# Gated linear attention inside a three-block kernel: the seven score levels of a 128-token tile become three levels of four blocks and one halving

## What is computed

```python
proj = h @ w_in                                    # q, k, v, r, gk_low; 4 heads, keys 128 wide, values 256 wide
log_a = log_sigmoid(gk_low @ w_gk_up + b_gk) / 16.0
b = cumsum(log_a) within a chunk
o_inter = einsum(q * exp(b), state)
attn[i, j] = sum_k q[i, k] * k[j, k] * exp(b[i, k] - b[j, k])   for j <= i
o_intra = attn @ v
state = state * exp(b_last) + (k * exp(b_last - b)).T @ v
y = (rms_norm(o_inter + o_intra) * silu(r)) @ w_out
```

## Time and profile before

| | us |
|---|---|
| median of three runs | 2564.52 |
| profiled execution, device time | 2564.55 |
| its span, first to last instruction | 2562.7 |
| GLA from t = 4 of head 1 to its last attend, 1532.58 to 1770.23 | 237.65 |
| of it TensorE busy | 237.65 |

### The profile page before, as it was taken

One profiled execution on the slowest core, in us unless ns is written; L12 is line 12 of the kernel. 1 busy time (PEld: TensorE's weight loads), 2 busy tenths in 40 slices (PEclk: granted clock), 3 DMA queues, 4 the chain that ended last, 5 costly groups with the idle time before them and its releaser, 6 DMA issues.

```text
span 2562.7 us, 34944 instructions
## 1 busy us (share of the span) xinstructions
PE 2527.1 (99%) x12568; PEld 2131.8 (83%) x12568; DVE 1220.7 (48%) x2483; ACT 922.5 (36%) x1840; POOL 467.0 (18%) x934
## 2 busy tenths in 40 slices
PE   8999999999999999999899999999999999999999
PEld 7888888888888987788788888888888888888887
DVE  4553634536423410577755767765443333333334
ACT  5443433324313422555544545443331122112212
POOL 3453534434000304322010001101000000000001
PEclk9999999999999999999999999999999999999999
DMA  6220212202533121222343111123331111111111
GB/s 211 78 76 22 93 36 64 67 27 85 192 115 111 63 95 48 60 60 60 98 146 113 40 61 34 41 74 114 109 140 41 50 57 41 47 44 64 33 49 74
DMA packets 76232, 194.48 MB, mean 76 GB/s; under 512 B 8528, under 2 KB 29392, under 8 KB 75344
## 3 DMA queue, kind: packets, MB, share of 16 engines
q1 hardware_dynamic: 76112, 192.85, 22.8%
HBM read 152.45 MB, written 36.18 MB: 74 GB/s over the span
## 4 chain that ended last, share of the span: by engine, by line
PE 58%; DVE 2%; issue 1%; ACT 1%; DMA 0%; POOL 0%; DVEq 0%; ACTq 0%; POOLq 0%
PE wc_g_ps L3431 14%; PE wc_y_ps L3447 14%; PE gl_vr_ps L2568 7%; PE gl_j_ps L2527 3%; PE wb_y_ps L2898 3%; PE wc_y_ps L3180 3%; PE gl_l_ps L2594 2%; PE at_T_ps L1931 1%; PE at_j_ps L1886 1%; PE at_v_ps L1886 1%; PE at_j_ps L1887 1%; PE at_j_ps L1888 1%; PE at_v_ps L1887 1%; PE at_v_ps L1888 1%; PE at_s_ps L1888 1%
## 5 line engine op out<-in xcount | busy, mean ns | idle before, releaser
L3431 PE MATMUL wc_g_ps<-x_upper,ff_w1l 128*128 128x512 f32 x512 | 199.3, 389 | 0.0
L3431 PE MATMUL wc_g_ps<-x_upper,ff_w1h 128*128 128x512 f32 x512 | 199.2, 389 | 0.0
L3447 PE MATMUL wc_y_ps<-ff_w2h,ff_hl 128*128 128x512 f32 x512 | 199.2, 389 | 0.0
L3447 PE MATMUL wc_y_ps<-ff_w2l,ff_hh 128*128 128x512 f32 x512 | 199.2, 389 | 0.0
L3431 PE MATMUL wc_g_ps<-x_lower,ff_w1h 128*128 128x512 f32 x512 | 199.2, 389 | 0.0
L3447 PE MATMUL wc_y_ps<-ff_w2h,ff_hh 128*128 128x512 f32 x512 | 199.2, 389 | 0.0
L3385 DVE TENSOR_TENSOR ff_acc<-wc_y_ps,ff_acc 128x1024 f32<-128x1024 f32 x63 | 77.2, 1225 | 210.9 <-PE wc_y_ps L3447 210.9
L3310 ACT ACTIVATE ff_relu<-wc_g_ps 128x512 f32<-128x512 f32 x64 | 38.3, 598 | 379.4 <-PE wc_g_ps L3431 379.4
L3371 DVE SCALAR_TENSOR_TENSOR wc_g_ps<-wc_g_ps,ff_relu 128x512 f32<-128x512 f32 x64 | 44.8, 700 | 178.7 <-ACT ff_relu L3310 178.7
L3339 POOL TENSOR_SCALAR ff_ms<-ff_ss 128x1 f32<-128x1 f32 x8 | 1.8, 223 | 686.9 <-ACT x_lower L3327 686.0
L3447 PEld LDWEIGHTS wc_y_ps<-ff_w2h,ff_hl 128*128 128x128 f32 x512 | 96.1, 188 | 20.0
(11 more groups left out here) (442 smaller groups left out, 6998.2 us busy)
## 6 DMA issues: line engine op xcount, KB each, us to landing
staging<-in_w_ff SPq DMA_DIRECT2D x64, 512.0 KB, 3.7
ra_raw<-in_w_wide_a SPq DMA_DIRECT2D x24, 512.0 KB, 3.7
ra_raw<-in_w_narrow_a SPq DMA_DIRECT2D x16, 512.0 KB, 3.7
staging<-in_w_vr_c SPq DMA_DIRECT2D x16, 512.0 KB, 3.9
wa_gin<-gated_a SPq DMA_DIRECT2D x6, 1024.0 KB, 4.9
ra_first_raw<-in_w_wide_a SPq DMA_DIRECT2D x8, 512.0 KB, 8.0
ra_x_rows<-in_x SPq DMA_DIRECT2D x8, 512.0 KB, 5.3
gated_a<-ra_sg SPq DMA_DIRECT2D x32, 128.0 KB, 2.0
```

Of the source, the lines that this page charges most:

```text
L3431: last = pe.matmul(f_ps[j % 2][:, :], a[kt // 2][:, kt % 2, f * P:(f + 1) * P], b[:, kt, half * HALF:(half + 1) * HALF], start=(kt == 0 an ...
L3447: last = pe.matmul(y_ps[t % 2][:, n, :], a[:, f, t * P:(t + 1) * P], b[f][:, n * HALF:(n + 1) * HALF], start=(f == 0 and i == 0), stop=(f ...
```

## The change

Six of the seven levels are joined by two: blocks of 1, 4 and 16 tokens, in groups of four blocks. Within a group every later block is scored against each earlier one, with reference r = 0, 1, 2 the last token of block r. The queries behind reference r are 96, 64 and 32 columns for a tile, 192 for each level; the keys of a level need one row of 128. For blocks of one token the keys are k itself. One halving (64 against 64) is left. The diagonal is taken from a product of k and q as they are, 128 columns. The exponents of a half are now 3·4·192 + 2·512 + 512 = 3840 instead of 4096, and `KD` moves to `lv_rest`, in place of q·k. Since k and q are now read directly and are overwritten for the next head before the last tiles are scored, tiles 4 to 7 get copies, `own_qk`. Four instructions of 256 elements make them in `products(h, 1)`. The scores lie in `l_ps` (128 + 192 + 192) and in `T_ps` (192 + 64 + 128 for the transpose). `gather_weights` has eleven parts in place of eight. The square in `output` now writes to `o_ps` instead of `osq`, whose place the copies take, and `attend` waits for `sq_done` instead of `o_copied`. In the closing product row 3 waits also for the scores of the last head's tile 3, and some tiles of the closing product and the feed-forward network change places.

```diff
-GLA_LEVELS = 7
+GLA_BLOCKS = (1, 4, 16)
+GLA_HALF = 64
...
+    BY_REF = (0, 96, 160)
+    QUERIES = 192
+    PARTS = 3 * NL + 2
+    LEVEL_AT = (P, P + QUERIES, 0)
+    HALVES_AT, KEYS_AT = QUERIES, QUERIES + GLA_HALF
...
+    def by_reference(c, level, r):
+
+        n = GLA_BLOCKS[level]
+        return queries(c, level)[:, :, BY_REF[r]:BY_REF[r] + 32 * (3 - r)].rearrange("p t (g x) -> p t g x", x=(3 - r) * n)
...
-            act.activation(lv_main[c][:, :, :], lv_main[c][:, :, :], ACT.Exp, scale=INV_NORM)
+            act.activation(lv_main[c][:, :], lv_main[c][:, :], ACT.Exp, scale=INV_NORM)
+            act.activation(lv_rest[c][:, 1, :], lv_rest[c][:, 1, :], ACT.Exp, scale=INV_NORM)
...
-            act.activation(osq[:, :], oS[:, t % 2, :], ACT.Square, accum_out=so[:, t % 2:t % 2 + 1]).then_inc(sq_done, 1)
+            act.activation(o_ps[:, 0:GV], oS[:, t % 2, :], ACT.Square, accum_out=so[:, t % 2:t % 2 + 1]).then_inc(sq_done, 1)
...
-            for level in range(NL):
-                n = 1 << level
-                src = b[:, at].rearrange("p (g u n) -> p g u n", u=2, n=n)
-                dst = lv_main[c][:, level, :].rearrange("p (g u n) -> p g u n", u=2, n=n)
-                mid = src[:, :, 0, n - 1:n].broadcast_to([P, HALF // (2 * n), n])
-                dve.tensor_tensor(dst[:, :, 0, :], mid, src[:, :, 0, :], ALU.subtract)
-                dve.tensor_tensor(dst[:, :, 1, :], src[:, :, 1, :], mid, ALU.subtract)
+            for level, n in enumerate(GLA_BLOCKS):
+                if level:
+                    src = b[:, at].rearrange("p (g n) -> p g n", n=n)
+                    dve.tensor_tensor(keys(c, level).rearrange("p (g n) -> p g n", n=n),
+                                      src[:, :, n - 1:n].broadcast_to([P, HALF // n, n]), src, ALU.subtract)
+                for r in range(3):
+                    src = b[:, at].rearrange("p (t g x) -> p t g x", t=BT, x=4 * n)
+                    dve.tensor_tensor(by_reference(c, level, r), behind_reference(b[:, at], level, r),
+                                      src[:, :, :, (r + 1) * n - 1:(r + 1) * n].broadcast_to([P, BT, 32 // n, (3 - r) * n]),
+                                      ALU.subtract)
...
+            if c:
+                for src in (q, k):
+                    for i in range(2):
+                        dve.tensor_copy(own_qk[src is k][i][:, :, :],
+                                        src[:, HALF + 2 * i * P:HALF + 2 * (i + 1) * P].rearrange("p (t n) -> p t n", n=P))
+            dve.tensor_tensor(lv_rest[c][:, 1, :], lv_rest[c][:, 1, :], k[:, at], ALU.mult)
+            dve.tensor_tensor(lv_rest[c][:, 0, :], lv_rest[c][:, 0, :], q[:, at], ALU.mult).then_inc(mul_done, 1)
...
+            dve.copy_predicated(aT_parts[0][:, :], ident[:].bitcast(U32), l_ps[:, 0:P]).then_inc(part_done, 1)
+            dve.copy_predicated(aT_parts[1][:, GLA_HALF:], mask[:, MASK_AT[-1]:MASK_AT[-1] + 1].broadcast_to([P, GLA_HALF]),
+                                T_ps[:, HALVES_AT:HALVES_AT + GLA_HALF]).then_inc(part_done, 1)
+            i = 2
+            for level, n in enumerate(GLA_BLOCKS):
+                bank, groups = (l_ps, l_ps, T_ps)[level], P // (4 * n)
+                for r in range(3):
+                    dve.wait_ge(part_done, PARTS * s + i - 1)
                     wait_alone(dve)
+                    at, x, w = LEVEL_AT[level] + BY_REF[r], (3 - r) * n, MASK_AT[level] + r * groups
+                    dve.copy_predicated(
+                        aT_parts[i % 2][:, :].rearrange("p (g x) -> p g x", x=4 * n)[:, :, (r + 1) * n:],
+                        mask[:, w:w + groups].unsqueeze(2).broadcast_to([P, groups, x]),
+                        bank[:, at:at + groups * x].rearrange("p (g x) -> p g x", x=x)).then_inc(part_done, 1)
+                    i += 1
...
             if older:
-                pe.wait_ge(o_copied, s)
+                pe.wait_ge(sq_done, s)
                 pe.wait_ge(R_done, s)
...
-            pe.matmul(T_ps[:, 0:P], ones[:, :], lv_rest[c][:, 1, at], start=True, stop=True)
-            pe.transpose(T_ps[:, P:2 * P], lv_main[c][:, KD, at], ident[:])
+            qc, kc = own_chunk(q, t), own_chunk(k, t)
+            pe.transpose(T_ps[:, KEYS_AT:KEYS_AT + P], lv_rest[c][:, 1, at], ident[:])
+            pe.matmul(l_ps[:, 0:P], kc, qc, start=True, stop=True)
             for level in range(NL):
...
+                pe.matmul((l_ps, l_ps, T_ps)[level][:, LEVEL_AT[level]:LEVEL_AT[level] + QUERIES],
+                          keys(c, level)[:, at] if level else kc, queries(c, level)[:, t % BT, :], start=True, stop=True)
+            last = pe.matmul(T_ps[:, HALVES_AT:HALVES_AT + GLA_HALF], halves(c)[:, at],
+                             halves(c)[:, t % BT * P + GLA_HALF:(t % BT + 1) * P], start=True, stop=True)
             last.then_inc(score_mm, 1)
...
             act.wait_ge(gl.mul_done, 2 * GLA_HEADS)
+            act.wait_ge(gl.score_mm, GLA_HEADS * NT - 4)
```

More of the change, by code:

```diff
@@ L2012, in gla_masks @@
 def gla_masks():
[L2017 to L2021, removed]
+    out = np.zeros((P, P), np.uint32)
+    token = np.arange(P)[:, None]
+    at = 0
+    for n in GLA_BLOCKS:
+        groups = P // (4 * n)
+        for r in range(3):
+            out[:, at:at + groups] = token // n == 4 * np.arange(groups)[None, :] + r
+            at += groups
+    out[:GLA_HALF, at] = 1
     return out
@@ L2045, in gla_heads @@
     KB = 1024
-    NL = GLA_LEVELS
-    KD = NL
+    NL = len(GLA_BLOCKS)
+    BY_REF = (0, 96, 160)
[3 more added lines that the diff above has]
+    HALVES_AT, KEYS_AT = QUERIES, QUERIES + GLA_HALF
+    MASK_AT = [3 * sum(P // (4 * m) for m in GLA_BLOCKS[:i]) for i in range(NL + 1)]
     BT = NT // 2
@@ L2082, in gla_heads @@
     ones = place("gl_ones", [P, P], F32, 76 * KB)
-    mask = place("gl_mask", [P, NL, P // 2], U32, 76 * KB + 512)
+    mask = place("gl_mask", [P, P], U32, 76 * KB + 512)
     so = place("gl_so", [P, 8], F32, 79 * KB + 832)
@@ L2114, in gates_of, with queries, keys, halves @@
         return slice(half * HALF, (half + 1) * HALF), half + 1
+    def queries(c, level):
+        at = level * BT * QUERIES
+        return lv_main[c][:, at:at + BT * QUERIES].rearrange("p (t n) -> p t n", t=BT)
+    def keys(c, level):
+        at = NL * BT * QUERIES + (level - 1) * HALF
+        return lv_main[c][:, at:at + HALF]
+    def halves(c):
+        return lv_main[c][:, EXPONENTS - HALF:EXPONENTS]
+    def own_chunk(src, t):
+        if t >= NT - 4:
+            return own_qk[src is k][t // 2 - 2][:, t % 2, :]
+        return src[:, t * P:(t + 1) * P]
+    def by_reference(c, level, r):
+        n = GLA_BLOCKS[level]
+        return queries(c, level)[:, :, BY_REF[r]:BY_REF[r] + 32 * (3 - r)].rearrange("p t (g x) -> p t g x", x=(3 - r) * n)
+    def behind_reference(src, level, r):
+        n = GLA_BLOCKS[level]
+        return src.rearrange("p (t g x) -> p t g x", t=BT, x=4 * n)[:, :, :, (r + 1) * n:]
     def gate_bank(half, first):
@@ L2410, in products @@
             for level in range(NL):
[L2411 to L2418, removed]
+                if level:
+                    dve.tensor_tensor(keys(c, level), keys(c, level), k[:, at], ALU.mult)
+                for r in range(3):
+                    dst = by_reference(c, level, r)
+                    dve.tensor_tensor(dst, dst, behind_reference(q[:, at], level, r), ALU.mult)
+            dst = halves(c).rearrange("p (t u n) -> p t u n", u=2, n=GLA_HALF)
+            for u, src in enumerate((k, q)):
+                dve.tensor_tensor(dst[:, :, u, :], dst[:, :, u, :],
+                                  src[:, at].rearrange("p (t u n) -> p t u n", u=2, n=GLA_HALF)[:, :, u, :], ALU.mult)
+            if c:
[5 more added lines that the diff above has]
+            dve.tensor_tensor(lv_rest[c][:, 0, :], lv_rest[c][:, 0, :], q[:, at], ALU.mult).then_inc(mul_done, 1)
         def carry_state(s, t, older):
@@ L2936, in gla_closing @@
     gh = [place(f"wc_gh{i}", [P, KW, P], F32R, at * KB) for i, at in enumerate((148, 156))]
-    glo = [place(f"wc_gl{i}", [P, KW, P], F32R, at * KB) for i, at in enumerate((152, 160))]
+    glo = [place(f"wc_gl{i}", [P, KW, P], F32R, at * KB) for i, at in enumerate((152, 164))]
     xin = place("wc_xin", [P, 2, DM], F32, 112 * KB)
@@ L3219, in feed_forward @@
     w1h = [place(f"ff_w1h{n}", [P, 2, HALF], F32R, at * KB) for n, at in enumerate((72, 76, 128, 148))]
-    w1l = [place(f"ff_w1l{n}", [P, 2, HALF], F32R, at * KB) for n, at in enumerate((164, 192, 144, 152))]
+    w1l = [place(f"ff_w1l{n}", [P, 2, HALF], F32R, at * KB) for n, at in enumerate((160, 192, 144, 152))]
     hh = place("ff_hh", [P, FT, SEQ], F32R, 80 * KB)
@@ L3224, in feed_forward @@
     w2l = [place(f"ff_w2l{f}", [P, DM], F32R, at * KB) for f, at in enumerate((140, 184, 68, 188))]
-    acc = [place(f"ff_acc{t}", [P, DM], F32, at * KB) for t, at in enumerate((156, 160, 112, 116, 120, 124, 172, 176))]
```

(1 more changed line is left out.)

40 lines of the change are left out of this document (16 added, 24 removed).

## The result

The changed kernel takes 2570.51 us, the kernel before 2565.34 on the same chip: a ratio of 1.0020, 95% interval 1.0013 to 1.0027. It is 5.2 us slower. The interval leaves out a ratio of 1, but the difference is only 0.2%, the size that the prediction took for the limit of what a measurement can tell.

A forecast was written before the change was run, and what follows sets the result against it. TensorE, busy 99% of the span, was taken as the bound. Three head cycles +1.2 us, last head from t = 4 +0.7, four steps left -1.2: +0.7 on the profiled 2564.55 gives 2565.2 us; range 2556 to 2572.

The forecast's parts named there:

- TensorE's saving: Scores on TensorE: 1.50 us instead of 1.81, saving 0.31 a step, 10 us over 32 steps.
- the slope: Matmul price of 0.84 ns per moving column, from 0.215 us for 256; gives 0.161 us for 192 columns.
- columns decide: Rival: TensorE pays by moving columns alone, scores +0.32 us a step, about 2580 us; chance 0.02.
- VectorE's and ScalarE's additions: Longer work per head: gather +0.55 us, exponents +0.2, products +0.5 on VectorE; exponentials +0.3 on ScalarE.
- the lower of my two values: VectorE's four copies in the products: about 0.22 us each, against 0.34 by the two-source rows.
- First wait, t = 5: TensorE's attend at t = 5 waits for ScalarE's square: 1.7 us in each head, 1.94 more in the last.
- t = 6: TensorE's attend at t = 6, behind VectorE's gather: no wait, but only 0.3 us spare.
- Second wait, head start: TensorE's first tile of heads 1 to 3 waits for VectorE's last weight piece: 1.2 us, three times.
- three places where TensorE arrives soon after what it waits for: Places checked for lateness: attend at t = 5, attend at t = 6, the first tile of the next head.
- its signs of being wrong: Scores not 1.5 us, no idle TensorE in GLA, gather 3 us or over, wait at t = 6 or 7, clock under 1.00.
- The gather costs twice: Rival: 0.05 us more per part, VectorE's gather grows by 1.05 us, time 2571.7 us; chance 0.20.
- Thin waits: Rival: gather, exponents and Exp no longer, first wait 0.6 us, second gone, 2557.2 us; chance 0.18.

The follow-up runs named there:

- e5: Changed kernel with piece 3 ahead of the exponentials, gates behind the output of tile 3, and second-half exponents at t=2; 2554.38 us, ratio to before 0.9960.
- e4: Changed kernel with VectorE's exponents of the second half at t=2 instead of t=3; 2560.43 us, ratio to the kernel before 0.9982.
- e1: Changed kernel with the square written as bf16 to a 512-byte place of its own and attend again waiting for the copy alone; 2568.29 us.
- e3: Changed kernel with ScalarE's gates of the next head queued at t=6 behind the output of tile 3, instead of at t=5 ahead of it; 2566.03 us.
- e6: Kernel before with the same three moves as e5; 2564.87 us, ratio 1.0000.
- e7: Kernel before with the square written into the outputs' bank and attend waiting for it instead of the copy; 2566.28 us.

## Why the prediction came out as it did

**The time.** 2570.5 lies inside the range, 5.3 above the forecast; against the kernel before, 0.7 was forecast and 5.2 measured. The mechanism was right (the saving on TensorE is given back as waiting), and a third wait was missed. That the range held is in part luck: its upper end, 2572, was the price of a gather of 3.05 us, which did not come, and the missed wait used the room.

**TensorE's saving.** Forecast 1.50 for the scores and 0.31 a step, measured 1.44 and 0.357 (91.13 - 88.27 = 2.86 for eight tiles, e5). The instruction of 192 columns came out at the 0.16 of the slope: 0.65 us for four (1540.34 to 1540.99), 0.163 each, and those of 64 and 128 columns at 0.065 to 0.115. The saving is 11.4 us in 32 steps, not 10. The rival "columns decide" is dead; the rule that the prediction set beside it (the Trainium skill, VectorE: DVE Perf Modes, "The TRN2 errata", a constant plus the columns) would give 192 columns, by an estimate from its figures, 198 cycles or 0.083 us at 2.4 GHz; the rows show twice that, and the measurement decides.

**VectorE's and ScalarE's additions.** Forecast gather +0.55, exponents +0.2, exponentials +0.3, products +0.5. Measured +0.57, +0.28, +0.31 (4.15 to 4.46, from the start of the Exp to the start of the copy of v behind the exponentials, 1546.20 above) and +0.49 (6.51 to 7.00). That copy in the kernel before, whose Exp starts at 1540.50:

```profile
1544.65 0.37 ACT L2245 ACTIVATE gl_v<-gl_vr_ps 128x256 f32<-128x256 f32 x1
```
The copies took 0.2 each, the lower of my two values. The rule that the prediction set beside them (the Trainium skill, VectorE: DVE Perf Modes, "What auto-detection actually checks", two elements a cycle for one source and SBUF on both sides, if the outer sizes are even or equal) fits: 256 elements of a product, with two sources, take 0.33 to 0.34 from start to start in the same stretch.

**First wait, t = 5.** Forecast 1.7 in heads 0 to 2; measured 1.70 from start to start in head 1, against e4. e4 takes it away. From the read of the sum to attend it is 0.10, where the prediction allowed 0.05. The sum gave the change of semaphore 0.54 of the 1.7, and e1 takes 0.55 away at this place. What the sum could not show is that this share is mostly lent: of the 0.87 that e1 takes at t = 5 and t = 7 of head 1, 0.50 comes back at t = 6 and the head start. In the last head 1.94 was forecast and 2.10 measured (10.41 from start to start, where a step that waits for nothing takes 8.31 there): the sum took 0.16 of waiting for already there in the kernel before, and its trace has 0.02 (8.70 against 8.68).

**t = 6.** Forecast no wait and 0.3 spare; measured none. The step is 0.08 longer than in e5, about the slow first pair behind the wait at t = 5. e1 used up the spare, as it had to.

**Second wait, head start.** Forecast 1.2, three times; measured 1.36 in head 1 against e5 (31.43 - 30.07). That the two are close is luck. The forecast is for a TensorE that did not wait at t = 7, and in that state, e3, the wait is 1.77 (31.84 - 30.07); in the changed kernel the missed wait holds TensorE back and hides 0.41 of it. The term that was too small is above all the gather of a head's last tile: forecast 2.55, it takes 2.89 in the changed kernel (1570.65 to 1573.54) and 2.88 in e3, where the same gather took 2.0 before. In it two parts start 0.53 apart that elsewhere start 0.18 apart:

```profile
1571.66 0.31 DVE L2514 COPY_PREDICATED gl_aT_even<-gl_mask,gl_l_ps 128x32 f32<-128x32 uint32 x1
1572.19 0.27 DVE L2514 COPY_PREDICATED gl_aT_odd<-gl_mask,gl_l_ps 128x96 f32<-128x96 uint32 x1 [0.22 <-DVE gl_aT_even L2514]
```
Why they do was not tested.

**The step that failed** is the count of places: "in three places where TensorE arrives soon after what it waits for". There is a fourth, attend at t = 7. The prediction listed a wait there among its signs of being wrong, but had not timed it. On ScalarE the output of tile 3 is queued behind the gates of the next head, which wait for VectorE's split. The kernel before at that place, where TensorE's attend starts at 1564.58:

```profile
1563.88 0.38 ACT L2255 ACTIVATE gl_oS<-gl_o_ps 128x256 f32<-128x256 f32 x1
1564.30 0.42 ACT L2257 ACTIVATE gl_osq<-gl_oS 128x256 f32<-128x256 f32 x1
1564.62 0.19 ACT L2257 ACTIVATION_READ_ACCUMULATOR gl_osq<-gl_oS 128x1 f32 x1
```
The copy ended at 1564.26, attend came at 1564.58: 0.3 to spare. By the prediction's own method the chain moves by VectorE's 2.1 and the square's 0.55, TensorE by 0.77, and the wait is 2.1 + 0.55 - 0.3 - 0.77 = 1.6. Measured 1.65 in head 1, and e3 takes it away alone. A head's cycle was forecast at +0.4 and came out at +1.93: +1.65 for this wait, +0.16 at the head start, +0.08 at t = 6, and -0.38 for the scores. Up to the last attend the changed kernel is 4.5 us later (1773.25 against 1768.74) where 0.7 was forecast: 4.8 for the three waits at t = 7, some 0.5 for t = 6, the head starts and t = 5 of the last head, 1.5 less for the scores. Of the 5.5 us between the profiled executions the last 1.0 lies behind GLA. The waits view has it in one place: TensorE's first transpose of the closing product's `wc_xn` waits 1.2 us for VectorE in the changed kernel and 0.2 in the kernel before. But the same wait is 0.8 in e6 and 0.9 in e7, which keep the levels of the kernel before, so that it belongs to the change is not shown.

**The rivals.** "The gather costs twice" named nearly the right time, 2571.7, by a price that wasn't there: the gather is 2.58, not 3.05, and 2.89 in a head's last tile alone. "Thin waits" fell with the same row. Had I timed the fourth place, the sum would have been near 2569 (an estimate: three times 1.65 less the 0.41 that e3 gives back, on top of 2565.2). The clock did not fall: over the stretches with the waits at t = 5, t = 7 and the head start (1548 to 1552, 1566 to 1570, 1592 to 1596) the granted clock reads 1.00.

## What to carry to other kernels

Where one engine is busy all the time, list every wait of that engine in one round of the loop with its spare before the change, not only the ones that the change edits; in this kernel the spares at the three places that came to wait were 0.25, 0.3 and 0.5 us, and 1.6 to 2.7 us of new lateness (longer work on VectorE and ScalarE, and before attend the later semaphore) passed through all of them. Shortening the full engine eats these spares from the other side. The remedy that paid was not less work but the order in the queues: three pieces of work with slack, moved one step, brought 16 us here and nothing to the kernel that had no waits.

## What the runs showed of the hardware

- A float32 matmul of 192 columns with weights that change every time takes 0.163 us, one of 64 or 128 between 0.065 and 0.115, one of 256 0.215: between a floor and a slope. For the last pair the floor is under my 0.106 (1541.32 to 1541.45 for two of 64 columns).
- ScalarE's square of 256 elements lasts 0.39 us written to PSUM and 0.42 written to SBUF, there in f32 and in bf16 (e1) alike. From its start to the start of the read of its sum it is 0.32 in both kernels (1548.55 to 1548.87; 1547.01 to 1547.33 before), so the engine gains nothing by the place.
- A GpSimd operation on one element a lane takes 0.19 us as a rule (the median of its 32), 0.49 beside a single gating operation of VectorE, and 4.34 when it falls into VectorE's products (3.83 before, where they were shorter). In both kernels it then ends 0.05 us behind the last product: 1553.56 against 1553.51, and before 1551.51 against 1551.46. VectorE waited 0.33 us for what GpSimd makes of it.

```profile
1549.22 4.34 POOL L2358 TENSOR_SCALAR gl_mo<-gl_so 128x1 f32<-128x1 f32 x1 [15.42 <-ACT gl_o_ps L2300]
...
1554.28 0.49 POOL L2358 TENSOR_SCALAR gl_mo<-gl_so 128x1 f32<-128x1 f32 x1
```
```profile
1554.23 0.49 DVE L2493 SCALAR_TENSOR_TENSOR gl_sr<-gl_oS,gl_ro,gl_sr 128x256 f32<-128x256 f32 x1 [0.33 <-POOL gl_ro L2361]
```
